# Gated linear layer: scaled keys and queries of the halves of 64 and of 32 side by side in one product

## The reference, cut to what matters

```python
def step(S, blk):                       # blocks of 16 tokens
    b = jnp.cumsum(gc, axis=-2)
    diff = b[..., :, None, :] - b[..., None, :, :]
    decay = jnp.exp(jnp.where(mask, diff, -jnp.inf))
    A = jnp.einsum('bhtd,bhsd,bhtsd->bhts', qc, kc, decay)
    o = A @ vc + (qc * jnp.exp(b)) @ S
    ...
```

## Time and profile before

| | |
|---|---|
| median of 3 runs | 1878.57 us (1877.97 to 1878.68) |
| the profiled execution | 1877.52 us, of it 1875.8 us span |
| granted TensorE clock, mean | 0.998 |
| busy share | PE 99%, PEld 83%, DVE 67%, ACT 51% |
| matmul records of the levels, L2634 and L2629 | 448 and 32 |

### The profile page before, as it was taken

The page is one execution under the profiler, slowest core; times in us unless marked ns, Lnnn a source line. Parts: engine busy times, 40 slices in busy tenths (PEclk is TensorE's granted clock), DMA queues, the critical chain, the costliest instruction groups (busy, mean ns, idle before and its releaser), DMA issues.

```text
span 1875.8 us, 24810 instructions
## 1 busy us (share of the span) xinstructions
PE 1853.0 (99%) x9049; PEld 1558.7 (83%) x9049; DVE 1255.0 (67%) x1684; ACT 955.7 (51%) x1336; POOL 27.4 (1%) x106
## 2 busy tenths in 40 slices
PE   8999999999999999999999999999999999999999
PEld 7788888778888888887888888888878888888887
DVE  6566666677557755658777777777767555677764
ACT  4455554355455546536554454544435444565542
POOL 4000000000000000000000000000000000000000
PEclk9999999999999999999999999999999999999999
DMA  6655454478789877565544454444446666545453
GB/s 234 202 172 147 135 168 144 148 212 184 181 155 211 181 180 169 196 238 155 160 160 153 148 170 145 151 162 157 147 159 196 188 187 186 167 152 168 155 170 114
DMA packets 170205, 319.27 MB, mean 170 GB/s; under 512 B 16600, under 2 KB 20848, under 8 KB 169344
## 3 DMA queue, kind: packets, MB, share of 16 engines
q1 hardware_dynamic: 168992, 313.70, 57.4%
q10 hardware_dynamic: 576, 4.19, 0.5%
q0 software_dynamic: 544, 0.13, 0.0%
HBM read 315.88 MB, written 2.10 MB: 170 GB/s over the span
## 4 chain that ended last, share of the span: by engine, by line
PE 48%; DVE 1%; issue 1%; ACT 1%; DVEq 0%; ACTq 0%
PE acc L287 14%; PE acc L289 14%; PE acc L288 14%; PE ps L2634 3%; PE ps L538 1%; PE ps L2618 0%; DVE arena L2005 0%; PE ps L2715 0%; PE ps L381 0%; PE ps L2608 0%; ACT whi L249 0%; PE ps L571 0%; ACT arena L1294 0%; DVE arena L1994 0%; DVE arena L1995 0%
## 5 line engine op out<-in xcount | busy, mean ns | idle before, releaser
L257 DVE TENSOR_TENSOR wlo<-wraw,whi 128x1024 fp32r<-128x1024 f32 (+3 forms) x616 | 713.8, 1177 | 414.5 <-ACT whi L249 411.6
L249 ACT ACTIVATE whi<-wraw 128x1024 fp32r<-128x1024 f32 (+3 forms) x616 | 614.5, 1017 | 330.8 <-PE acc L289 326.0
L287 PE MATMUL acc<-whi,ta_hi 128*128 128x512 f32 x1664 | 659.9, 397 | 3.6 <-DVE wlo L257 3.5
L289 PE MATMUL acc<-whi,ta_lo 128*128 128x512 f32 x1664 | 648.7, 390 | 0.0
L288 PE MATMUL acc<-wlo,ta_hi 128*128 128x512 f32 x1664 | 648.0, 389 | 0.0
L287 PEld LDWEIGHTS acc<-whi,ta_hi 128*128 128x128 f32 x1664 | 312.7, 188 | 69.4 <-DVE wlo L257 4.4
L289 PEld LDWEIGHTS acc<-whi,ta_lo 128*128 128x128 f32 x1664 | 312.4, 188 | 66.6
L288 PEld LDWEIGHTS acc<-wlo,ta_hi 128*128 128x128 f32 x1664 | 312.9, 188 | 61.9
L287 PE MATMUL acc<-whi,tb_hi 128*128 128x512 f32 (+1 forms) x704 | 277.1, 394 | 1.1 <-DVE wlo L257 1.1
L289 PE MATMUL acc<-whi,tb_lo 128*128 128x512 f32 (+1 forms) x704 | 271.3, 385 | 0.0
L288 PE MATMUL acc<-wlo,tb_hi 128*128 128x512 f32 (+1 forms) x704 | 271.0, 385 | 0.0
(11 more groups left out here) (310 smaller groups left out, 1303.8 us busy)
## 6 DMA issues: line engine op xcount, KB each, us to landing
wraw<-in_ml_w_in SPq DMA_DIRECT2D x128, 512.0 KB, 6.0
wraw<-in_a_w_in SPq DMA_DIRECT2D x128, 512.0 KB, 4.0
wraw<-in_kv_w SPq DMA_DIRECT2D x64, 512.0 KB, 4.5
wraw<-in_b_w_in SPq DMA_DIRECT2D x64, 512.0 KB, 4.3
wraw<-in_mla_w_in SPq DMA_DIRECT2D x48, 512.0 KB, 4.9
wraw<-in_mla_w_out SPq DMA_DIRECT2D x32, 512.0 KB, 4.0
wraw<-in_ml_w_out SPq DMA_DIRECT2D x32, 512.0 KB, 4.5
wraw<-in_a_w_out SPq DMA_DIRECT2D x32, 512.0 KB, 4.4
```

What stands on the lines that cost most here:

```text
L249: nc.scalar.activation(whi[:, n % SPLIT, :, 0:w], wraw[:, n % RAW, :, 0:w], ACT.Copy).then_inc(w_high, 1)
L257: nc.vector.tensor_tensor(wlo[:, n % SPLIT, :, 0:w], wraw[:, n % RAW, :, 0:w], whi[:, n % SPLIT, :, 0:w].bitcast(F32), ALU.subtract).then_ ...
L287: nc.tensor.matmul(o, xh, wh, start=first, stop=False)
L289: m = nc.tensor.matmul(o, xl, wh, start=False, stop=end)
```

## The change

The levels j = 1 (halves of 64) and j = 2 (halves of 32) get one product. The keys of level 1 take columns 0 to 63 of each 128-block of a new tile `dM` (level 1's decays are computed there), those of level 2 columns 64 to 127; the queries likewise in a new `qM`. Eight matmuls of 128x128 give all pairs of these; of the result three blocks are of use, and DVE copies them from PSUM into `aT`, two of them to other partitions than they were computed on (64 to 95 goes to 0 to 31, 96 to 127 goes to 64 to 95). No mask is needed for them. There are now 7 steps: step 0 is level 0, step 1 the joined product, step i > 1 level i + 1. The table loses the entry 25, so the joined product stands after unit 27, where level 2 stood, and the later levels stay where they were. On ACT and DVE all that a step prepares is one level further ahead: three distances and three pairs of exponentials in `diag`, four multiplications in step 0 (`scale_two`), and unit 28 has no side work left.

```diff
-        L2_AT = {..., "diag": 21, "level": [23, 25, 27, 29, 31, 33, 35, 37], "gate": 38, "pv": 39,
+        L2_AT = {..., "diag": 21, "level": [23, 27, 29, 31, 33, 35, 37], "gate": 38, "pv": 39,
+        dM, qM = A(8, P), A(8, P)
+        STEPS = 7
+        HALF = (P, 64, 32, 16, 8, 4, 2, 1)
+        def decay_of(j):
+            return dM.rearrange("p n t -> p (n t)") if j == 1 else dT[:, (0, 0, 1, 0, 1, 0, 1, 0)[j], :]
...
 # ACT
                     decays(0)
                     decays(1)
+                    decays(2)
-                        decays(j + 2)
+                        decays(i + 3)
...
 # DVE
+                def scale_two():
+                    d, e = flat(dM), decay_of(2)
+                    quarters = lambda v, c: v.rearrange("p (n m c r) -> p n m c r", m=2, c=2, r=32)[:, :, :, c, :]
+                    behind = lambda v: v[:, :, 64:].rearrange("p n (m r) -> p n m r", r=32)
+                    dve.wait_ge(l2["ee"], 4 + 16 * g)
+                    nc.vector.tensor_tensor(dM[:, :, 0:64], dM[:, :, 0:64], half(flat(kT2), 0, 64), ...)
+                    nc.vector.tensor_tensor(qM[:, :, 0:64], dM[:, :, 64:], half(flat(qT2), 1, 64), ...)
+                    dve.wait_ge(l2["ee"], 6 + 16 * g)
+                    dve.wait_ge(l2["op"], 4 + 16 * g)
+                    nc.vector.tensor_tensor(behind(dM), quarters(e, 0), quarters(flat(kT2), 0), ...)
+                    nc.vector.tensor_tensor(behind(qM), quarters(e, 1), quarters(flat(qT2), 1), ...)
...
                     distance(0)
                     distance(1)
+                    distance(2)
...
-                def level(j):
-                    scale(j + 1)
-                    dve.wait_ge(l2["lv"], j + 1 + 8 * g)
+                def level(i):
+                    if i == 0:
+                        scale_two()
+                    else:
+                        scale(i + 2)
+                    dve.wait_ge(l2["lv"], i + 1 + STEPS * g)
...
+                    elif i == 1:
+                        m = ps2(0).rearrange("p (n t) -> p n t", t=P)
+                        nc.vector.tensor_copy(aT[0:64, :, 64:128], m[0:64, :, 0:64])
+                        nc.vector.tensor_copy(aT[0:32, :, 32:64], m[64:96, :, 64:96])
+                        nc.vector.tensor_copy(aT[64:96, :, 96:128], m[96:128, :, 96:128]).then_inc(l2["sel"], 1)
...
-                    distance(j + 2)
+                    distance(i + 3)
...
 # PE
+                def level(i):
+                    pe.wait_ge(l2["op"], scaled_after(i, g))
+                    if i == 1:
+                        pe.wait_ge(l2["at"], 1 + g)
+                        for n in range(8):
+                            m = nc.tensor.matmul(ps2(0)[:, n * P:(n + 1) * P], dM[:, n, :], qM[:, n, :], ...)
+                        m.then_inc(l2["lv"], 1)
+                        return
```

More of the change, by code:

```diff
@@ L777, in free_l2 @@
                     eng.wait_ge(l2["ogp"], TB * it)
-        L2_AT = {"turn": 16, "decay": 18, "diag": 21, "level": [23, 25, 27, 29, 31, 33, 35, 37], "gate": 38, "pv": 39,
+        L2_AT = {"turn": 16, "decay": 18, "diag": 21, "level": [23, 27, 29, 31, 33, 35, 37], "gate": 38, "pv": 39,
                  "norm": 39, "back": 42}
@@ L787, in group, with step_of, scaled_after @@
             return slice(first + n * g, first + n * g + n) if isinstance(g, int) else bass.ds(first + n * g, n)
+        STEPS = 7
+        HALF = (P, 64, 32, 16, 8, 4, 2, 1)
+        def step_of(j):
+            return (0, 1, 1, 2, 3, 4, 5, 6)[j]
+        def decay_of(j):
+            return dM.rearrange("p n t -> p (n t)") if j == 1 else dT[:, (0, 0, 1, 0, 1, 0, 1, 0)[j], :]
+        def scaled_after(s, g):
+            return (2 if s == 0 else 4 + 2 * s) + 16 * g
         def heads_of(t, g, b):
@@ L1328, in l2_side @@
                     diag()
-                for j in range(8):
-                    if u == L2_AT["level"][j] + LAG:
-                        decays(j + 2)
+                for i in range(STEPS):
+                    if u == L2_AT["level"][i] + LAG:
+                        decays(i + 3)
                 if u == L2_AT["gate"] + LAG:
@@ L2032, in scale @@
                         return
-                    h = P >> j
+                    h, d = HALF[j], decay_of(j)
                     dve.wait_ge(l2["ee"], 2 * j + 2 + 16 * g)
@@ L2110, in l2_side @@
                     diag()
-                for j in range(8):
-                    if u == L2_AT["level"][j] + LAG:
-                        level(j)
+                for i in range(STEPS):
+                    if u == L2_AT["level"][i] + LAG:
+                        level(i)
                 if u == L2_AT["gate"] + LAG:
@@ L2620, in diag @@
                     m.then_inc(l2["dg"], 1)
[L2622 to L2626, removed]
+                def level(i):
[3 more added lines that the diff above has]
+                        for n in range(8):
+                            m = nc.tensor.matmul(ps2(0)[:, n * P:(n + 1) * P], dM[:, n, :], qM[:, n, :], start=True,
+                                                 stop=True)
+                        m.then_inc(l2["lv"], 1)
+                        return
+                    if i >= 2:
+                        pe.wait_ge(l2["sel"], i - 1 + STEPS * g)
+                    k = decay_of(i + 1 if i else 0).rearrange("p (h t) -> p h t", t=T)
+                    q = qx[:, i % 2, :]
                     for h in range(4):
-                        if j == 0:
-                            m = nc.tensor.matmul(ps[:, 2, h * P:(h + 1) * P], k[:, h, 0:P],
-                                                 qx[:, 0, h * P:(h + 1) * P], start=True, stop=True)
+                        if i == 0:
+                            m = nc.tensor.matmul(ps[:, 2, h * P:(h + 1) * P], k[:, h, 0:P], q[:, h * P:(h + 1) * P],
+                                                 start=True, stop=True)
                             continue
@@ L2633, in level @@
                             n = 2 * h + b
-                            m = nc.tensor.matmul(ps[:, 2 + j % 2, n * 64:(n + 1) * 64], k[:, h, b * P:(b + 1) * P],
-                                                 qx[:, j % 2, n * 64:(n + 1) * 64], start=True, stop=True)
+                            m = nc.tensor.matmul(ps[:, 2 + i % 2, n * 64:(n + 1) * 64], k[:, h, b * P:(b + 1) * P],
+                                                 q[:, n * 64:(n + 1) * 64], start=True, stop=True)
                     m.then_inc(l2["lv"], 1)
                 def values():
-                    pe.wait_ge(l2["sel"], 8 + 8 * g)
+                    pe.wait_ge(l2["sel"], STEPS + STEPS * g)
                     landed(pe, "l2", 2, g)
@@ L2660, in l2_side @@
                     diag()
-                for j in range(8):
-                    if u == L2_AT["level"][j]:
-                        level(j)
+                for i in range(STEPS):
+                    if u == L2_AT["level"][i]:
+                        level(i)
                 if u == L2_AT["pv"]:
```

48 lines of the change are left out of this document (28 added, 20 removed).

## The result

The changed kernel takes 1881.08 us, the median of 20 runs (1878.44 to 1882.17), against 1878.43 us of the kernel before in as many runs (1877.52 to 1879.18). The ratio is 1.0013 with a 95% interval of 1.0007 to 1.0019: slower by a hair, and within the 0.2% that I had called no change. The forecast was 1880.9 us.

A forecast was written before the change was run, and what follows sets the result against it. PE bounds on average, fed by a slower DVE and ACT chain whose lead runs out; 0.60 + 0.07 - 0.10 = 0.57 us a group, 2.3 us in four, on 1878.57 us gives 1880.9 us, range 1877.4 to 1884.4 us.

The forecast's parts named there:

- The sum on PE: PE's matmuls: joining costs 0.07 us and saves a level of 1.80 us, net 1.73 us a group if nothing waits.
- What is put ahead of unit 27's `low`: DVE: third distance 1.14, two more multiplications 1.20, wait on itself 0.11 us; that `low` comes 2.45 us later.
- the rival of the dear multiplications: DVE's `scale_two`: four multiplications at 0.21 us more each, 0.82 us a group, giving 1884.2 us; chance 0.20.
- Where PE meets it: PE at level 0 starts 0.94 us late, then waits a further 1.46 us and starts unit 27 0.60 us late.
- The joined product's follow-up: PE behind unit 27: the joined product adds 0.07 us, leaving PE 0.67 us behind before.
- What follows is covered: Units 28 to 31: DVE and ACT 1.7 us ahead of before, lead 2.4 us larger, copies 1.3 us covered.
- the 0.10 us at the group's end: PE's wait at the last two levels, 7.36 us apart instead of 7.26; forecast to vanish.
- The sum: Whole group: 0.60 + 0.07 - 0.10 = 0.57 us more, 2.3 us in four groups, forecast 1880.9 us.
- The gain that did not arrive: Rival at PE: no wait at unit 27, the saved level arrives in full, 1871.3 us; chance 0.07.
- The clock: Rival at PE's new waits: the clock falls for 6 us each time, 2.6 us a group, 1891 us; chance 0.03.

The follow-up runs named there:

- both moves: Changed kernel, third distance put behind level 0's scaling, level 2's two multiplications and level 3's distance behind unit 27's `low`: 1871.25 us, ratio 0.9964 to before.
- one more instruction in unit 28: Changed kernel plus one unread DVE sum over 128x1024 (about 1.15 us) a group, put into unit 28: 1880.74 us, ratio 1.0014 to before.
- the late distance: Changed kernel with the third distance behind level 0's scaling instead of ahead of the diagonal, level 2's decays at unit 26: 1880.48 us, ratio 1.0014.

## Why the prediction was right

**The sum on PE.** The join was to cost 0.07 us and save 1.80 us. It costs 0.00 (above). I had read the 1.78 us of `diag` as the price of 128 columns. But `diag` starts behind a wait, and that is what it pays for: level 0 too takes 0.92 us to the next product behind its wait (1037.75 to 1038.67 us), and 0.81 us without one in the kernel with both moves (1033.36 to 1034.17 us). The joined product lasts 1.95 us and not 2.02 us. The net saving came out as 1.76 us in the kernel with both moves (1.73 us forecast), which is near by luck: the level behind the joined product comes 1.80 us sooner behind `diag` than before (26.41 against 28.21 us), and the difference is lost to PE's wait at the group's end, which the sum did not have.

**What is put ahead of unit 27's `low`.** Forecast 1.14 + 1.20 + 0.11 = 2.45 us, measured 17.54 - 15.01 = 2.53 us. The distance took 1.14 us and each multiplication 0.60 to 0.61 us from start to start, in strips of 64 and runs of 32 too, as their rows said; DVE's wait on itself is 0.18 us a step and not 0.11 us. So the rival of the dear multiplications is out.

**Where PE meets it.** Level 0 late by 0.94 us forecast, 0.84 us measured; unit 27 late by 0.60 us forecast, 0.59 us measured. At level 0 the error is the hand-over from DVE to PE: 0.06 us (1037.01 + 0.68 to 1037.75 us), where I had taken 0.15 us from `diag`. The agreement at unit 27 is luck, two errors that cancel: `low` comes 0.08 us later than forecast, and the hand-over is again 0.06 us (1047.12 + 1.22 to 1048.40 us). The profile's idle of 0.68 and 1.30 us begins at the end of the last product, 0.39 us behind its start, where the next would have started 0.23 us behind it; so the delay at level 0 is 0.16 us more than its idle.

**The joined product's follow-up.** Forecast 0.67 us late behind it, measured 0.72 us. The 0.07 us was wrong in its cause; in its place unit 27 itself is slower behind a wait: 2.86 us to the joined product (1048.40 to 1051.26 us), where a unit in full flow took 2.73 us.

**What follows is covered.** The three copies took 1.59 us with the distance behind them at its place (1.3 us forecast), the `low` of unit 31 starts 28.64 us behind `diag`, where it was 29.98 us before:

```profile
1057.40 2.36 DVE L257 TENSOR_TENSOR wlo<-wraw,whi 128x1024 fp32r<-128x1024 f32 x2 [2.17 <-ACT whi L249]
```

So the chain is 1.3 us ahead of before there (1.7 us forecast), and PE 0.72 us behind it: a lead 2.1 us larger and not 2.4 us. It was enough: the last two levels are 7.26 us apart, and the 0.10 us at the group's end are gone. The kernel with one more instruction in unit 28 shows that this stretch has room for 1.2 us more.

**The sum.** 0.57 us a group forecast, 0.63 us measured; 2.3 against 2.65 us in the medians and 2.45 us in the profiles' stretch behind the first `diag`.

**The gain that did not arrive.** Its rival had 1871.3 us, 7.3 us less, and both moves show that it was there to be had: 9.8 us between the changed kernel and the one with both moves, with the same matmuls. That the 1871.25 us of both moves meet the rival's time is luck in part: the rival counted the 0.10 us at the group's end as gone, and there they stay. What kept it was where two of four multiplications and one distance stood.

**The clock.** The rival was dismissed with the argument that an idle of 1.6 us had left the clock up. That argument was weak: in the changed kernel's own profiled execution the same idle was followed by 0.86. In the third layer the waits of 1.30 us left it at 1.00 in the profile; longer ones, from 1.9 us up, did not always (below).

## What to carry to other kernels

Before taking work off the busiest engine, find the hand-overs that feed it, and count what the edit puts ahead of each: here two engines with a third and half of their time idle decided the result, since each `low` waits behind side work in a fixed order. When a step is joined with the next one, its preparation need not stand in one piece; it can be laid behind the next thing that the bound engine needs. And a wait behind which a longer one follows is worth nothing until that is gone, so moves like these are judged together.

## What the runs showed of the hardware that was not expected

The granted clock can fall behind a wait that is far shorter than the 3.59 us of the earlier trace rows, in a stretch where PE has no other gap over 0.7 us. Behind waits of 1.30 us at unit 27 it stayed up in four of four groups of the profiled execution; behind 2.24 us it fell in one of four (the kernel with the late distance), behind 1.9 us in one of four, behind 2.4 us in three of four. The same idle of 1.6 us near 855 us was followed by a fall in the profiled executions of two kernels, the change and the late distance, and by none in the other ten. Each fall costs 1.5 to 1.6 us here. So a wait can cost more than its length, and not each time the same: 1.1 us more of it cost 2.0 us a group in the median.

A step of 16 matmul records of 4-byte operands takes 1.7 us with 64 and with 128 columns. Copies from PSUM to other partitions took 0.42 and 0.43 us for 32 partitions x 256, one of them from partitions 64 to 95 to 0 to 31, the other from 96 to 127 to 64 to 95. A copy from PSUM of 8 partitions x 256 that changes no partition took 0.41 us in the same trace (L1828), so the move costs next to nothing.
